# Second weight pair of two projection layers: where the first pair's results go, and the order in which the token sums are made and split

## The reference, cut to what matters

```python
def even_layer(x, norm_g, w_in, pool_w, pool_scale, ws, bs, w_out):
    h = rmsnorm_2(x, norm_g)
    z = h @ w_in
    a, g_a, u, v, g_b = jnp.split(z, [...], axis=-1)
    y_a = multiscale_pool(a, pool_w, pool_scale) * jax.nn.silu(g_a)
    ...

def odd_layer(x, norm_g, w_in, conv_w, w_out):
    h = rmsnorm_2(x, norm_g)
    z = h @ w_in
    qkv, g_c, d_b, d_c, d_x, g_d = jnp.split(z, [...], axis=-1)
    ...                                  # dilated group attention on qkv
```

## Time and profile before

| | us |
|---|---|
| median of 3 runs | 3255.93 (3255.35 to 3257.89) |
| the profiled execution | 3259.52 |
| its span in the trace | 3257.8 |
| PE busy | 3126.4 (96% of the span) |
| DVE, ACT, POOL busy | 1628.6, 1413.5, 1601.6 |
| mean granted clock of PE | 0.982 of full |

### The profile page before, as it was taken

How to read it: one execution, slowest core, us unless ns; L and a number is a source line. 1 busy time by engine, 2 the same in 40 slices (tenths; PEclk the granted TensorE clock), 3 DMA queues, 4 the chain that set the end, 5 groups by cost and what they waited for, 6 DMA issues and landing times. The chain is left out here.

```text
span 3257.8 us, 43754 instructions
## 1 busy us (share of the span) xinstructions
PE 3126.4 (96%) x16354; PEld 2596.7 (80%) x16354; DVE 1628.6 (50%) x2387; ACT 1413.5 (43%) x2391; POOL 1601.6 (49%) x1040
## 2 busy tenths in 40 slices
PE   6989999889899989999999999999999999999998
PEld 4777888766788868788888788888888888888887
DVE  5366623855799776623523644444444444334622
ACT  5156323723677743333301545455445445333311
POOL 2331333042221249977633656556556556788732
PEclk8999999989899989999999999999999999999999
DMA  8230212173999952222522111111111111222322
GB/s 295 56 86 27 56 33 88 31 262 120 342 402 393 359 161 81 78 85 65 179 80 80 34 55 43 56 46 50 48 46 53 46 49 49 81 75 66 134 88 71
DMA packets 321602, 362.42 MB, mean 111 GB/s; under 512 B 28679, under 2 KB 288683, under 8 KB 315124
## 3 DMA queue, kind: packets, MB, share of 16 engines
q1 hardware_dynamic: 309774, 319.74, 29.4%
q0 software_dynamic: 4896, 16.78, 2.0%
q10 hardware_dynamic: 6726, 23.13, 1.8%
HBM read 297.48 MB, written 58.72 MB: 109 GB/s over the span
## 5 line engine op out<-in xcount | busy, mean ns | idle before, releaser
L2989 POOL TENSOR_TENSOR quarter_lo<-quarter_w_sums,quarter_hi 128x512 fp32r<-128x512 f32 x296 | 425.1, 1443 | 232.4 <-ACT quarter_hi L2984 230.4
L2989 POOL TENSOR_TENSOR quarter_lo<-quarter_raw,quarter_hi 128x512 fp32r<-128x512 f32 x222 | 313.8, 1413 | 279.6 <-ACT quarter_hi L2984 273.2
L3078 PE MATMUL odd_z<-odd_t_hi,quarter_hi 128*128 128x512 f32 x780 | 324.9, 416 | 9.3 <-ACT dil_set L3046 7.9
L2984 ACT CAST quarter_hi<-quarter_w_sums 128x512 fp32r<-128x512 f32 x296 | 184.6, 624 | 315.4 <-PE first_z L3080 157.2
L3078 PE MATMUL first_z<-odd_t_hi,quarter_hi 128*128 128x512 f32 x760 | 316.1, 416 | 0.0
L3080 PE MATMUL odd_z<-odd_t_hi,quarter_lo 128*128 128x512 f32 x780 | 306.0, 392 | 0.0
L3079 PE MATMUL odd_z<-odd_t_lo,quarter_hi 128*128 128x512 f32 x780 | 304.5, 390 | 0.0
L3080 PE MATMUL first_z<-odd_t_hi,quarter_lo 128*128 128x512 f32 x760 | 297.7, 392 | 0.0
L3079 PE MATMUL first_z<-odd_t_lo,quarter_hi 128*128 128x512 f32 x760 | 296.2, 390 | 0.0
L276 POOL TENSOR_TENSOR w_hi<-w_raw,zero_col 128x1024 fp32r<-128x1024 f32 x25 | 49.9, 1994 | 289.6 <-DMA w_raw<-in_w_in 97.8
L2984 ACT CAST quarter_hi<-quarter_raw 128x512 fp32r<-128x512 f32 x222 | 138.1, 622 | 101.8 <-PE first_z L3080 50.4
(11 more groups left out here) (727 smaller groups left out, 8151.6 us busy)
## 6 DMA issues: line engine op xcount, KB each, us to landing
quarter_raw<-in_odd_w_in SPq DMA_DIRECT2D x224, 256.0 KB, 3.4
raw_gate<-in_w_gate SPq DMA_DIRECT2D x16, 2048.0 KB, 16.0
raw_up<-in_w_up SPq DMA_DIRECT2D x16, 2048.0 KB, 16.0
raw_down<-in_w_down SPq DMA_DIRECT2D x16, 2048.0 KB, 15.9
quarter_raw<-in_even_w_in SPq DMA_DIRECT2D x64, 256.0 KB, 3.2
start_w_mod<-in_w_mod SPq DMA_DIRECT2D x11, 1024.0 KB, 10.6
w_raw<-in_w_in SPq DMA_DIRECT2D x16, 512.0 KB, 3.7
mix_w_early<-in_w_mod SPq DMA_DIRECT2D x8, 1024.0 KB, 12.2
```

The lines of the kernel that those rows point to most:

```text
L2984: act.copy(self.w_hi[:, n % self.SLOTS], self.source(m, i)).then_inc(self.hi_done, 1)
L2989: pool.tensor_tensor(self.w_lo[:, n % self.SLOTS], self.source(m, i), self.w_hi[:, n % self.SLOTS].bitcast(F32), ALU.subtract).then_inc(se ...
L3078: pe.matmul(to, self.w_hi[:, slot, kt], t_hi[:, kt], start=(begins and kt == 0), stop=False, skip_group_check=True)
```

## The change

Both layers get the same edits, with differences named.

- Pair 0 is copied to a home of its own (`a_first`, `first_set`), which doesn't lie on the normed tokens. ACT no longer waits for T3's sum (nor, in the first layer, for the pad's memset) before these copies; there it waits for the stored tokens instead. The pads are cleared later, together (two memsets more).
- T2's raw sum goes to T4's place. DVE therefore waits for `quarters.product` at 5 ahead of T2's sum, where it waited ahead of T4's.
- DVE's order is now: T1 sum, T2 sum, T1 low, T2 low, T3 sum, T4 sum, T3 low, T4 low.
- ACT makes the high parts of T3 and T4 inside pair 1, behind `copy(1, 0)` and `copy(1, 1)`. In the second layer `copy(1, 0)` itself waits for T3's sum, since `sets[1]` lies on what that sum reads.
- Second layer only: T4's low part stands on DVE behind `bias(0, 0)` and `bias(0, 1)`.
- First layer only: SP doesn't wait for the scaling before it loads pair 1.

The diff, without the declarations of the homes and the removed semaphore:

```diff
@@ sync, first layer
                     sp.wait_ge(x_stored, 16 * GROUPS)
-                    sp.wait_ge(scaled_done, GROUPS)
@@ scalar, first layer
-                    for n, i in enumerate((T1_SUM, T2_SUM, T3_SUM, T4_SUM)):
-                        act.wait_ge(t_added, n + 1)
-                        token_hi(i, even_sums[i][:])
-                        if i == T3_SUM:
-                            act.wait_ge(pads_clear, 1)
-                            quarters.plain_copy(act, 0, banks, targets(0))
-                            quarters.plain_copy(act, 1, banks, targets(0))
-                            quarters.hi(act, 7)
-                            quarters.hi(act, 8)
+                    act.wait_ge(x_stored, 16 * GROUPS)
+                    plain_copied(0)
+                    plain_copied(1)
+                    quarters.hi(act, 7)
+                    quarters.hi(act, 8)
+                    act.wait_ge(t_added, 1)
+                    token_hi(T1_SUM, even_sums[T1_SUM][:])
+                    plain_copied(2)
                     quarters.hi(act, 9)
-                    quarters.plain_copy(act, 2, banks, targets(0))
-                    quarters.plain_copy(act, 3, banks, targets(0))
+                    plain_copied(3)
+                    act.wait_ge(t_added, 2)
+                    token_hi(T2_SUM, even_sums[T4_SUM][:])
                     quarters.hi(act, 10)
...
                         copy(m, 0)
+                        if m == 1:
+                            act.wait_ge(t_added, 3)
+                            token_hi(T3_SUM, even_sums[T3_SUM][:])
                         hi(m, 0)
...
                         copy(m, 1)
+                        if m == 1:
+                            act.wait_ge(t_added, 4)
+                            token_hi(T4_SUM, even_sums[T4_SUM][:])
                         hi(m, 1)
@@ vector, first layer
                     token_sum(T1_SUM, b12, b11)
                     dve.wait_ge(x_stored, 16 * GROUPS)
+                    dve.wait_ge(quarters.product, 5)
                     dve.wait_ge(t_added, 1)
-                    token_sum(T2_SUM, b22, even_sums[T1_SUM][:])
+                    dve.tensor_tensor(even_sums[T4_SUM][:], b22, even_sums[T1_SUM][:], ALU.subtract).then_inc(t_added, 1)
+                    token_lo(T1_SUM, even_sums[T1_SUM][:], 5)
+                    token_lo(T2_SUM, even_sums[T4_SUM][:], 6)
                     token_sum(T3_SUM, b22, b12)
-                    dve.wait_ge(t_added, 3)
-                    step = Steps(dve, dve_step)
-                    step(dve.memset(a_pad[0][:, :, 0:PAD], 0.0))
...
@@ scalar, second layer (the start as above, plain copies 0 and 1 between B12's and B22's high parts)
+                        if h == 0:
+                            act.wait_ge(t_added, 3)
                         copy(m + 1, 0)
+                        if h == 0:
+                            token_hi(T3_SUM, odd_sums[T3_SUM][:])
...
@@ vector, second layer (sums and low parts as above)
-                        bias(h, 0, 1, 2)
+                        if h == 0:
+                            dve.wait_ge(t_added, 4)
+                        bias(h, 0, 1)
+                        if h == 0:
+                            token_lo(T4_SUM, odd_sums[T4_SUM][:], 10)
+                        bias(h, 2)
```

More of the change, by code:

```diff
@@ L3225, in phase_even @@
             t_lo_done = sem("even_t_lo_done")
-            pads_clear = sem("even_pads_clear")
             dve_step = sem("even_dve_step")
@@ L3281, in targets @@
                 if m < POOL_PAIRS and m % 2 == 0:
-                    return [[a_pad[m // 2 % 2][:, t, PAD + b * HALF:PAD + (b + 1) * HALF] for b in range(2)] for t in range(2)] + [lambda bank: bank]
+                    a = a_pad[m // 2 % 2] if m else a_first
+                    return [[a[:, t, PAD + b * HALF:PAD + (b + 1) * HALF] for b in range(2)] for t in range(2)] + [lambda bank: bank]
                 to = silu if m < POOL_PAIRS else (v_cm, g_cm, u_cm)[(m - POOL_PAIRS) % 3]
@@ L3740, in _ @@
                     dve.wait_ge(x_stored, 16 * GROUPS)
+                    dve.wait_ge(quarters.product, 5)
                     dve.wait_ge(t_added, 1)
-                    token_sum(T2_SUM, b22, even_sums[T1_SUM][:])
+                    dve.tensor_tensor(even_sums[T4_SUM][:], b22, even_sums[T1_SUM][:], ALU.subtract).then_inc(t_added, 1)
+                    token_lo(T1_SUM, even_sums[T1_SUM][:], 5)
+                    token_lo(T2_SUM, even_sums[T4_SUM][:], 6)
                     token_sum(T3_SUM, b22, b12)
-                    dve.wait_ge(t_added, 3)
-                    step = Steps(dve, dve_step)
-                    step(dve.memset(a_pad[0][:, :, 0:PAD], 0.0))
-                    step.wait()
-                    dve.sem_inc(pads_clear, 1)
-                    token_lo(T1_SUM, even_sums[T1_SUM][:], 5)
-                    dve.wait_ge(quarters.product, 5)
-                    token_sum(T4_SUM, b21, even_sums[T2_SUM][:])
-                    dve.wait_ge(t_added, 4)
-                    token_lo(T2_SUM, even_sums[T2_SUM][:], 6)
+                    token_sum(T4_SUM, b21, even_sums[T4_SUM][:])
                     token_lo(T3_SUM, even_sums[T3_SUM][:], 7)
                     token_lo(T4_SUM, even_sums[T4_SUM][:], 8)
+                    step = Steps(dve, dve_step)
                     def join(m, i):
@@ L3766, in pool_part @@
                             t, k = n // each, n % each
-                            a = a_pad[g % 2][:, t]
+                            a = (a_pad[g % 2] if g else a_first)[:, t]
                             now = a if k == 0 else sums[:, (k - 1) % 2]
@@ L3824, in _ @@
                             step(dve.memset(sums[:, :, 0:PAD], 0.0))
+                            step(dve.memset(a_first[:, :, 0:PAD], 0.0))
+                            step(dve.memset(a_pad[0][:, :, 0:PAD], 0.0))
                             step(dve.memset(a_pad[1][:, :, 0:PAD], 0.0))
@@ L3951, in phase_odd @@
             probs = [mem(f"dil_p{u}", [P, n * P]) for u, (_, _, _, n) in enumerate(units)]
+            first_at = probs_at + sum(n for _, _, _, n in units[:BLOCKS]) * P * 4
+            first_set = Arena(nc, first_at)("dil_first_set", [P, 2, SEQ])
+            assert max(odd_x_at + (KT + 1) * SEQ * 4, first_at) + 2 * SEQ * 4 <= mem.at
             neg_max = mem("dil_neg_max", [P, NU])
@@ L4099, in set_of @@
             def set_of(h, j):
-                return sets[(h * HEAD_PAIRS + j) % 2]
+                return sets[(h * HEAD_PAIRS + j) % 2] if h or j else first_set
             with nc.psum_tensor("odd_z", [P, 2, HALF], F32) as second_z, nc.psum_tensor("odd_aux", [P, 2, HALF], F32) as aux, \
```

42 lines of the change are left out of this document (24 added, 18 removed).

## The result

| | before | changed |
|---|---|---|
| median of 13 runs each, in turns on one chip | 3256.49 us | 3263.51 us |
| lowest to highest | 3254.21 to 3262.63 | 3261.41 to 3267.39 |
| profiled execution | 3259.52 | 3267.39 |
| its span | 3257.8 | 3265.6 |
| mean granted clock | 0.982 | 0.982 |

The ratio is 1.0022, with a 95% interval of 1.0015 to 1.003: the change makes the kernel slower by 7.0 us (the medians; 7.2 by the ratio, whose interval is 4.9 to 9.8). PE's row of the page, against the earlier trace rows, has the same 96% and the same count of matmuls, and 2.0 us more of busy time.

A forecast was written before the change was run, and what follows sets the result against it. PE, busy 96% of the span, was taken as the bound, with at most some 13.8 us to be had. First layer +8.9 and second -1.9 gave +7.0, 3255.93 to 3262.9 us; 8-in-10 range 3251 to 3267.

The forecast's parts named there:

- Which places: PE's gaps: first layer 3.8 before (1,4), 6 before (1,6); second about 1 before (1,1), 5.0 before (1,2); none before (1,0).
- The price of a turn, 1.1: DVE chains in both layers: 2.2 for each DVE step, plus 1.1 for each POOL operation between.
- the rival in which DVE wins the turns: Both layers' DVE chains go at 2.2 to 2.7 a step: -3, 3253, or half-way +2, 3258; chance 0.20.
- `pool_part` up to join 4: First layer, DVE: work queued between the end of T4 low and the end of join 4, taken as 9.8.
- +8.9: First layer: (2,0) starts at 1241.7 against 1232.84, after stops before (1,4) and (1,6); ends +0 to +10.
- DVE's wait for product 5: First layer: DVE ends T1's sum at 1196.4 and stands until 1204.05 ahead of T2's sum, 7.6 us.
- Second layer: The 7.94 gap before (1,0) goes, (1,2) waits 5.0 for T3's sum through copy(1, 0): -1.9, ends -6 to +1.
- The rival that it doesn't fall: PE's clock stays up at the new stalls: first layer +7.2, second -3.6, sum +3.6, 3259.5; chance 0.10.

The follow-up runs named there:

- x2: Only the first layer's part of the change, made on the kernel before: ratio 1.0024 (1.0014 to 1.0033), +7.8 us against the kernel before.
- x1: Only the second layer's part of the change, made on the kernel before: ratio 0.9997 (0.9988 to 1.0006), -1.0 us against the kernel before.
- x10: The changed kernel with 12 more matmuls ahead of (1,4) and 27 ahead of (1,6) in the first layer: 1.0006, +2.0 us against the kernel before.

## Why the prediction was right

3262.9 was forecast and 3263.51 measured; for the profiled execution 3266.5 and 3267.39.

- *Which places.* The four idle times were named with their owners: 3.8 before (1,4) (3.81), 6 before (1,6) ended by a join (4.86, so 1.1 too long), 1 before (1,1) (0.95), 5.0 before (1,2) (4.75), and none before (1,0) in either layer. (1,2) starts 34.94 behind plain product 0 of its layer; forecast 34.9 (1813.3 - 1778.43).
- *The price of a turn, 1.1.* The four steps of 3.3 in a row are in the profile, and the run with little POOL work shows the cause. (The argument for the price said that before the change every step of this chain paid the 1.1; T4's sum didn't, it took 2.28.) From product 5 (1200.63 by the weight part on ACT that waits for it) to the end of T4 low 23.35 was forecast, and it is 23.3. Of the rival in which DVE wins the turns nothing is seen behind product 5. It does happen ahead of it, as in the earlier trace rows, where POOL waited through the rest of one step and through two whole ones (not three turns, as I wrote).
- *Term too large: `pool_part` up to join 4.* From the end of T4 low to that of join 4 I took 9.8, the 9.7 of before. It is 8.8, for the step of 1008 elements took 1.21, not 2.26. POOL was there, but it had the second turn: its low part began 0.02 behind this step and took 2.32 in place of 1.29. In the kernel before, POOL's low part began 0.10 ahead of the same step (1224.22), and DVE waited. After, then before:

```profile
1230.06 1.21 DVE L3785 SCALAR_TENSOR_TENSOR pool_pooled<-pool_sums,pool_a_first 128x1008 f32<-128x1008 f32 x1
1230.08 2.32 POOL L2989 TENSOR_TENSOR quarter_lo<-quarter_raw,quarter_hi 128x512 fp32r<-128x512 f32 x1
```

```profile
1224.32 2.26 DVE L3780 SCALAR_TENSOR_TENSOR pool_pooled<-pool_sums,pool_a 128x1008 f32<-128x1008 f32 x1
```

  That (-1.0) and a slow start of (1,6) of 4.15 in place of 4.4, against 0.3 more in plain products 1 to 4, make +8.0 of the +8.9.
- *Term that doesn't matter: DVE's wait for product 5.* 7.6 was forecast, 4.24 is in the profile. The three low parts ahead took 8.9 in place of 6.69, since POOL's sums for pair 1 now run beside them (I had put that at up to 1.1; it is 2.2), and plain product 0 had no slow start in this execution, as it had in the profile that the forecast was worked from (2.82 against 4.43). Nothing follows from it, as the chain starts with product 5. In x2, with a slow product 0, the wait was 7.40. Weight part 7, too, could be made from 1201.3 on, not 1201.95; nothing hangs on that either.
- *Second layer.* -1.9 forecast, -1.8 in the distances; in x1 alone -2.0.
- *Clock.* The rival that it doesn't fall is out: both stops of the first layer are followed by 1.4 more, and x10 gets the second one back.
- The sum of the two distances is +6.1 in the one profile and +7.2 in the other, and the time +7.0 and +5.5. The mechanism was right in both layers and each term within 1 us. That the forecast came within a microsecond of the median has some luck in it, for start and end of the program scatter by several: plain product 1 starts between 1180.1 and 1188.5 in the thirteen profiles.

## What to carry to other kernels

When a result is moved to another place, the wait that guards this place moves with it, and everything that is queued behind it on the engine: here one wait came two sums sooner and cost 8 us in one layer, most of it at a product that stood for a join of 0.7, and that join stood behind other work. Before an idle time is attacked, follow every engine that feeds the next ten products in its own order; each stop that was removed here brought another to light (behind the copy 3.8 and 4.9, behind the wait for product 5 1.95, behind the S4 sum 3.5, behind pair 2's sums 0.8), and only the version that reordered all of them was clearly faster. And where VectorE and GpSimd both work on SBUF in the same stretch, cost a chain in turns, not in the durations of either engine alone.
